# Five of eight blocks of the last layer's output projection as filler of the stick-breaking steps, whose tiles run from the last to the first

## What is computed

```
h = x @ w_in                      # split into q, k, v, gates of three mixers
o_nsa = nsa_mixer(...)            # 6 heads, columns 0:384
o_sb  = stick_breaking_mixer(...) # 4 heads, columns 384:640
o_hg  = hgrn2_mixer(...)          # 6 heads, columns 640:1024, a recurrence over the tokens
mixed = concat([o_nsa * silu(nsa_z), o_sb * silu(sb_z), norm(o_hg) * silu(hg_z)])
x = layer_norm(ALPHA * x + mixed @ w_out, ln_g, ln_b)
```

## Time and profile before

| | |
|---|---|
| median of 3 runs | 1381.4 us (1378.87 to 1387.62) |
| the profiled execution | 1383.62 us, its span 1381.8 us |
| mean granted TensorE clock | 0.925 |
| PE busy | 1223.5 us (89%) |
| DVE busy | 552.5 us (40%) |
| ACT busy | 427.6 us (31%) |
| POOL busy | 112.5 us (8%) |

### The profile page before, as it was taken

One profiled execution on the slowest core, in us unless ns is written; L12 is line 12 of the kernel. 1 busy time (PEld: TensorE's weight loads), 2 busy tenths in 40 slices (PEclk: granted clock), 3 DMA queues, 4 the chain that ended last, 5 costly groups with the idle time before them and its releaser, 6 DMA issues.

```text
span 1381.8 us, 15110 instructions
## 1 busy us (share of the span) xinstructions
PE 1223.5 (89%) x5264; PEld 684.8 (50%) x5264; DVE 552.5 (40%) x1422; ACT 427.6 (31%) x1086; POOL 112.5 (8%) x140
## 2 busy tenths in 40 slices
PE   4879989999898899979999989989999899867974
PEld 1555454455564444334455555555454556445541
DVE  3234323333544320334443432112225632758871
ACT  0133013444451101222234321114344544651211
POOL 0000000000002000000000000000000000574722
PEclk8889989999998999999999999999999999856997
DMA  9321234463002422332111005241101111000000
GB/s 347 105 92 31 93 127 177 160 226 73 0 1 70 77 38 61 70 111 61 62 61 61 1 11 137 62 167 46 46 1 46 46 62 62 1 3 30 1 32 30
DMA packets 60258, 99.71 MB, mean 72 GB/s; under 512 B 12068, under 2 KB 22129, under 8 KB 60184
## 3 DMA queue, kind: packets, MB, share of 16 engines
q1 hardware_dynamic: 54370, 93.58, 21.9%
q10 hardware_dynamic: 5814, 5.18, 1.2%
HBM read 96.60 MB, written 4.08 MB: 73 GB/s over the span
## 4 chain that ended last, share of the span: by engine, by line
PE 75%; DVE 13%; ACT 6%; issue 2%; DMA 2%; ACTq 1%; POOL 0%; DVEq 0%; SPq 0%; POOLq 0%
PE PR L867 33%; PE OB L897 6%; PE PT L779 6%; PE SC L919 6%; PE PR L779 5%; PE OB L779 4%; PE SC L779 4%; PE PT L934 3%; PE PR L960 3%; DVE stage L1677 2%; DMA ring<-in_w_ada 2%; DVE d L1677 1%; DVE tok L1677 1%; DVE arena L1893 1%; PE PT L867 1%
## 5 line engine op out<-in xcount | busy, mean ns | idle before, releaser
L867 PE MATMUL PR<-ring,hT 128*128 128x512 f32 (+1 forms) x784 | 381.7, 600 | 4.8 <-ACT hT L1208 4.0
L867 PEld LDWEIGHTS PR<-ring,hT 128*128 128x128 f32 x784 | 137.7, 199 | 105.0 <-issue 87.8
L1367 ACT ACTIVATE stage<-stage,nmax 128x256 f32<-128x256 f32 (+7 forms) x200 | 103.7, 519 | 264.7 <-DVE nmax L2023 233.5
L897 PEld LDWEIGHTS OB<-arena,pts 128*128 128x128 f32 (+3 forms) x880 | 133.1, 202 | 99.9 <-issue 76.8
L867 PE MATMUL PR<-hT,ring 128*128 128x512 f32 (+1 forms) x304 | 149.9, 616 | 0.0
L1585 POOL TENSOR_TENSOR arena<-arena 128x192 f32<-128x192 f32 (+1 forms) x118 | 80.1, 679 | 798.3 <-PE OB L897 749.5
L897 PE MATMUL OB<-arena,pts 128*128 128x64 f32 (+4 forms) x880 | 131.4, 279 | 11.5 <-ACT pts L1208 11.5
L919 PE MATMUL SC<-arena 64*128 64x256 f32 (+15 forms) x432 | 114.9, 459 | 10.2 <-DVE nmax L2023 10.2
L934 PEld LDWEIGHTS PT<-ident,stage 128*128 128x128 f32 (+3 forms) x440 | 59.1, 147 | 110.7 <-issue 69.0
L934 PE MATMUL PT<-ident,stage 128*128 128x128 f32 (+3 forms) x440 | 87.2, 290 | 24.6 <-ACT stage L1339 11.8
L1208 ACT ACTIVATE pts<-PT 128x256 f32<-128x256 f32 (+7 forms) x200 | 80.9, 404 | 84.0 <-PE PT L934 62.4
(11 more groups left out here) (337 smaller groups left out, 1288.5 us busy)
## 6 DMA issues: line engine op xcount, KB each, us to landing
ring<-in_w_ada SPq DMA_DIRECT2D x12, 2048.0 KB, 8.3
ring<-in_od_w_in SPq DMA_DIRECT2D x8, 2048.0 KB, 16.7
ring<-in_w_in SPq DMA_DIRECT2D x5, 1536.0 KB, 6.9
ring<-in_ev_w_in SPq DMA_DIRECT2D x3, 2048.0 KB, 7.7
ring<-in_w_in SPq DMA_DIRECT2D x3, 2048.0 KB, 10.0
ring<-in_ev_w_out SPq DMA_DIRECT2D x2, 2048.0 KB, 10.2
ring<-in_od_w_out SPq DMA_DIRECT2D x2, 2048.0 KB, 8.0
ring<-in_w_out SPq DMA_DIRECT2D x2, 2048.0 KB, 7.7
```

Of the source, the lines that this page charges most:

```text
L867: mm = pe.matmul(dst, l, r, start=(k == 0), stop=(k == KT - 1))
L897: mm = pe.matmul(ob[:, h * w:h * w + w], pts[0:rows_, v % 2, n * P:n * P + P], vb, start=(n == 0), stop=(n == len(blocks) - 1))
L1367: give(act.activation(pb[:, s % NP, 0:n], zm[:, s % 2, 0:n], ACT.Exp, bias=nmax[:, row, c:c + 1], scale=-1.0, accum_out=rsum[:, row, c:c + ...
```

## The change

Two things are done together.

1. The first five blocks of each tile's output projection leave `output_tile`. For each tile they become four jobs, `heads_ahead(i)`: `mE` 0 and 1 transpose the five finished blocks (4 and 1) and ACT copies them back into `tok`; `ye` 0 and 1 are the two halves of five products each, and DVE's `residual_ahead` writes `ALPHA * x + product` into `x`. Tiles 3, 2 and the first three jobs of tile 1 are filler of steps 78 to 87; tile 1's last job runs between attention and the tail; tile 0's four run beside c = 0 of the tail. `output_tile` keeps three transposes, one ACT copy and twice three products, and `residual_half` becomes a plain addition.
2. The stick-breaking groups run tile 3, 2, 1, 0 (`STICK_ORDER`). The earlier filler is moved into fewer steps: 21 tiles in steps 0 to 64, `hi` in steps 65 to 77. `HG_EARLY` stays (78, 84).

```diff
+EARLY = 5
+STICK_ORDER = (3, 2, 1, 0)
+def heads_ahead(i):
+    return [("mE", i, 0), ("mE", i, 1), ("ye", i, 0), ("ye", i, 1)]
...
-     (("w", "hi"), [("hi", i) for i in range(T)])],
+     (("w", "hi"), [("hi", i) for i in range(T)]),
+     (("wo", 2, 0), []),
+     (("wo", 2, 1), heads_ahead(3) + heads_ahead(2) + heads_ahead(1)[:3])],
...
-[(21, 68), (4, 14)]]
+[(21, 65), (4, 13), (2, 1), (2, 3), (2, 1), (2, 3), (2, 1), (1, 1)]]
...
+    jobs.append(("ye", 1, 1))
     for c in range(T + 1):
         if c < T - 1:
             jobs.append(("kbT", c))
         if c:
-            jobs.extend([("mT", 2, c - 1, 0), ("mT", 2, c - 1, 1), ("y", 2, c - 1, 0), ("y", 2, c - 1, 1)])
+            jobs.extend([("mT", 2, c - 1, 0), ("y", 2, c - 1, 0), ("y", 2, c - 1, 1)])
+        else:
+            jobs.extend(heads_ahead(0))
...
-OUT_SPREAD = [8, 4, 4, 8]
+OUT_SPREAD = [[5, 4, 3, 0], [3, 2, 2, 2]]
...
+                if kind == "mE":
+                    i, g = name[1:]
+                    if g == 0:
+                        pe.wait_ge(ob_free, g_no[2, 3 * T + STICK_ORDER.index(i)] + 1)
+                    transposes(name, [tok[:, i, k * P:k * P + P] for k in ((4,) if g else range(4))])
+                if kind == "ye":
+                    for g in range(2):
+                        freed(pe, ("mE", i, g))
+                    for k in range(EARLY):
+                        mm = pe.matmul(b[:, :], tok[:, i, k * P:k * P + P], W[:, k, :], ...)
...
-            drained(pe, ("hi", T - 1))
+            whole_tile(("ye", 1, 1))
             pe.wait_ge(ob_free, len(g_no))
...
+            def mixed_ahead(i, g):
+                b = take(act, ("mE", i, g))
+                release(copy(tok[:, i, 4 * P * g:4 * P * g + w], b[:, 0:w]), ("mE", i, g))
...
+            def residual_ahead(i, h):
+                b, w = take(dve, ("ye", i, h)), slice(512 * h, 512 * h + 512)
+                release(stt(x[:, i, w], x[:, i, w], ALPHA, b[:, :], ALU.mult, ALU.add), ("ye", i, h))
...
-                release(stt(ybuf2[:, i % 2, w], x[:, i, w], ALPHA, b[:, :], ALU.mult, ALU.add), ("y", 2, i, h))
+                release(tt(ybuf2[:, i % 2, w], x[:, i, w], b[:, :], ALU.add), ("y", 2, i, h))
...
-                    if c and m == 0:
-                        mixed_half(c - 1)
+                    if c == 0 and m == 0:
+                        residual_ahead(1, 1)
...
                 if c:
                     residual_half(c - 1, 0)
+                else:
+                    for h in range(2):
+                        residual_ahead(0, h)
```

More of the change, by code:

```diff
@@ L293, in attention_plan @@
             groups += [(kind, i, [[(kind, h, i)] for h in row_halves(NSH)]) for kind in ("cmp", "sel", "win")]
-        groups += [("sb", i, [[("sb", h, i)] for h in range(SBH)]) for i in range(T)]
+        groups += [("sb", i, [[("sb", h, i)] for h in range(SBH)]) for i in STICK_ORDER]
     return groups
-OUT_SPREAD = [8, 4, 4, 8]
+OUT_SPREAD = [[5, 4, 3, 0], [3, 2, 2, 2]]
 RING = 3
@@ L338, in two_block_kernel @@
     for name in jobs:
-        few = name in beside or name[0] in ("kbT", "st") or name[:2] in (("mT", 2), ("y", 2))
+        few = name in beside or name[0] in ("kbT", "st", "mE", "ye") or name[:2] in (("mT", 2), ("y", 2))
         b = turn[few] % (2 if few else 8)
@@ L943, in output_tile @@
             def output_tile(i):
[L945 to L955, removed]
+                b = begin(("mT", 2, i, 0))
+                for k in range(EARLY, KT):
+                    if k == EARLY:
+                        pe.wait_ge(hof, i + 1)
+                    tr = pe.transpose(b[:, (k - EARLY) * P:(k - EARLY + 1) * P], tok[:, i, k * P:k * P + P], ident[:, :])
+                    if k == KT - 1:
+                        tr.then_inc(pr_done, 1)
+                    yield
+                freed(pe, ("mT", 2, i, 0))
                 for h in range(2):
@@ L958, in output_tile @@
                     b = begin(("y", 2, i, h))
-                    for k in range(KT):
-                        mm = pe.matmul(b[:, :], hT[:, k, i * P:i * P + P], W[:, k, :], start=(k == 0), stop=(k == KT - 1))
+                    for k in range(EARLY, KT):
+                        mm = pe.matmul(b[:, :], hT[:, k, i * P:i * P + P], W[:, k, :], start=(k == EARLY), stop=(k == KT - 1))
                         if k == KT - 1:
@@ L1151, in outputs @@
                     mm.then_inc(ho_done, 1)
-                beside_it = output_tile(c - 1) if c else iter(())
+                beside_it = output_tile(c - 1) if c else (None for name in heads_ahead(0) for _ in tile_matmuls(name))
                 def feed(k):
-                    for _ in range(OUT_SPREAD[k]):
+                    for _ in range(OUT_SPREAD[min(c, 1)][k]):
                         next(beside_it, None)
@@ L1554, in _ @@
                     b = take(act, ("mT", 2, c - 1, 0))
-                    release(copy(hT[:, 0:4, (c - 1) * P:c * P], heads(b[:, :])), ("mT", 2, c - 1, 0))
+                    release(copy(hT[:, EARLY:KT, (c - 1) * P:c * P],
+                                 b[:, 0:384].rearrange("p (j t) -> p j t", j=KT - EARLY)), ("mT", 2, c - 1, 0))
+                else:
+                    for g in range(2):
+                        mixed_ahead(0, g)
                 if 1 <= c < T - 1:
@@ L1872, in tile_done @@
                     next(chains[-1])
+                elif kind == "ye":
+                    residual_ahead(*name[1:])
                 elif kind == "mT" and i == 1:
@@ L2228, in output_tile @@
                 give(ts(yb, yb, lam[:, 7:8], ALU.add, rr[:, 0:1], ALU.mult), ln_s, i + 1)
[L2230 to L2233, removed]
             def residual_half(i, h):
@@ L2293, in _ @@
             output_tile(T - 2)
-            mixed_half(T - 1)
             residual_half(T - 1, 0)
```

23 lines of the change are left out of this document (18 added, 5 removed).

## The result

| | before | changed kernel |
|---|---|---|
| median of 7 runs each, side by side | 1383.74 us (1378.83 to 1387.63) | 1391.2 us (1389.96 to 1397.69) |
| ratio, 95% interval | | 1.0069 [1.0051, 1.0086] |
| profiled execution, its span | 1383.62, 1381.8 us | 1390.36, 1388.6 us |
| mean granted clock | 0.925 | 0.931 |

The changed kernel is slower by 0.7%: the interval leaves 1 out, and the difference is less than the 1% that the prediction counted as telling. The forecast was 1388. Its span, 1388.6, is to the tenth that of the profiled execution, but this one is the second shortest of the seven; the median lies 3.2 us above the forecast, and the kernel before came out 2.3 us above the median that the forecast started from. By the ratio the change cost 9.5 us, where +6.8 was forecast.

The account below looks back on a forecast made before the run. The DVE-ACT ping-pong and POOL's chain were taken to bound the stick-breaking steps, mostly DVE the tail. +17.8 + 7.9 - 4.8 - 14.1 = +6.8 us gave 1388 us against the median 1381.4; 8 in 10 range 1369 to 1404.

Parts of the forecast that it names:

- Part 1: Before step 72: eight more filler products cost 5.2 us, longer scores of three units +1.9.
- Part 2: Step 72 to end of step 78: ping-pong sets the pace, PE's work is hidden; exponentials 0 start about 1210.4, 16.5 us later.
- Part 3: Steps 79 to tail: late POOL makes ACT stand some 5 us before exponentials 1 at 1238.7; whole stick-breaking part +17.8 us.
- the slower rival: Clock stays at 1.2 GHz through the `ye` filler: +17 on the forecast, 1405; chance 0.25.
- two signs of failure: Prediction fails if ACT meets no wait at step 84, or something other than the ping-pong paces the stick-breaking steps.
- the ping-pong: Stick-breaking steps: DVE and ACT alternate, unit r + 2's mask awaiting unit r's last exponential; period 4.57 us for 512 keys.
- Part 4: Tail, c = 0: waiting for a bank DVE frees, added products and a lower clock make 22 us of 14.1, +7.9.
- Part 5: Tail, c = 1 to 3: each loses DVE's 0.69 us copy into `hT`; -3.1, -0.7 and -1.0 us.
- Part 6: After the last tile's recurrence: 10.4 us instead of 24.5, six products 7.7 mostly at the lower clock; -14.1 us.
- Faster: Stick-breaking steps: POOL and ACT are done before PE needs them, the fill covers the gaps; 1365 to 1378, chance 0.20.
- No effect: Whole kernel: the work moved is hidden at both ends; inside the forecast's own range, no separate chance.

Follow-up runs that it names:

- v6: Changed kernel with tiles 1 and 2 left in the tail; tile 3's jobs in the steps, tile 0's beside c = 0: 1378.03 us, ratio 0.9970.
- v1: Kernel before, order and filler kept, only tile 3's four jobs made ahead, all beside c = 0: 1366.69 us, ratio 0.9892.
- v5: Kernel before, order reversed, tile 3's first three jobs in steps 82 to 87, its last beside c = 0: 1369.66 us, ratio 0.9905.
- e4: Changed kernel with other products placed between a tile's transposes and its own products: 1391.77 us, ratio 1.0058.
- e3: Changed kernel with exponentials 0 at the end of step 75 instead of 78: 1394.46 us, ratio 1.0075.
- e1: Kernel before with only the stick-breaking tiles reversed: 1382.52 us, ratio 1.0006.
- v3: Kernel before, tile 3's first three jobs beside c = 0, its last beside c = 2, tile 0's four in steps 82 to 87: 1366.39 us, ratio 0.9891.
- e2: Changed kernel with DVE's residual_ahead(1, 1) before the tail's loop, not after the first combination: 1387.03 us, ratio 1.0023.
- v2: Kernel before, only tile 3's jobs made ahead, the first three beside c = 0, the last beside c = 2: 1365.35 us, ratio 0.9882.
- v4: Kernel before, order reversed, old filler kept, only tile 3's four jobs ahead, in steps 82 to 87: 1366.26 us, ratio 0.9902.

## Why the prediction was right, and where it wasn't

**Part 1, the filler moved up.** Forecast were +5.2 for the filler and +1.9 for the scores, together 7.1. The changed kernel's profile alone shows +3.5; the twelve in groups show +6.0 and +2.0. The eight extra products in a stretch without a gap cost about what their durations say, and v6, which still pays them (and 6.1 us more in c = 0), is the one reduced version that stays behind v1 to v5.

**Part 2, the long steps first.** Exponentials 0 begin at 1208.95; 1210.4 was forecast. The error is in two terms that go against each other: P came 3.6 us earlier than forecast in this profile, and from P to the exponentials it took some 2 us longer.

**Part 3, the step that failed.** The forecast had POOL late and ACT standing still for 5 us in front of exponentials 1. ACT met no wait there, and it was POOL that stood still, for 7.51 us. Three terms were off. POOL took 22.3 us (21.37 and 0.83, with its gaps), not 24.5, so it was done at 1235.19, not 1238.7. ACT came at 1238.73, not 1234. And what follows exponentials 1 took 15.1 us (1242.55 to 1257.67), not 17.6, since the last ten products ran in about 9.2 us, near full clock, not mostly at the lower one. ACT was late because PE was: the sum for steps 79 to 84 had the products' durations and no term for the two waits for ACT's copies (2.72 and 2.73 us), nor for the six records behind each, which took 2.05 + 3.62 us where six take some 2.7 at full clock. That is 5.45 and about 6 us, more than the 4.7 us by which ACT was late, and no run took the waits away (e4 meant to and didn't, v6 keeps the first of them), so what each is worth is not shown. The forecast saw exactly this wait in c = 0 and in the slower rival's sentence, and left it out of the sum of the steps. An error of 3.5 us (POOL) and one of 4.7 (ACT) met at the same number, 1238.7, and the exponentials began there by luck. Of the two signs of failure that the prediction named for itself, the first came true outright (ACT met no wait at step 84). So did the second, in the steps after exponentials 0: not the ping-pong paced them but PE (DVE waits there for PE's scores, line 951, up to 6.9 us at a time). That the total was near doesn't make that step right. e3 settles which of the two it was: with POOL done 16.8 us ahead, nothing moved.

The mechanism isn't wrong as such. It is there in e1, v5 and v6 (ACT waits 2.50, 3.69 and 1.91 us). It needs PE to be quick, and with the new products PE isn't.

By the Trainium skill (SBUF — State Buffer, "SBUF: two separate sides"), named in Part 3, a POOL instruction that reads SBUF and a DVE instruction with two SBUF inputs exclude each other. POOL's 31 instructions took 26.9 us with the tiles in the old order and 22.3 in the changed kernel. Of the stretch of the first 30, DVE was busy 18.11 of 25.97 us before, 14.64 of 24.34 in v3, 13.70 of 21.57 in e1 and 10.94 of 21.37 in the changed kernel. POOL's first 15 took 10.22 us in the old order and 13.30 in e4, now beside the long steps. That agrees with the rule; no run here changed DVE's work alone.

**Part 4, c = 0.** +7.68, forecast +7.9, by the steps named: the wait for DVE's release (3.35 us) and the lower clock after it (six records in 4.83 us). e2 takes the wait away and gets 5.85 us back, so the cause is shown.

**Part 5.** c = 1 gained 2.95, forecast 3.1. c = 2 and c = 3 were to gain 0.7 and 1.0 and gained nothing (-0.13, +0.28). The step that failed is "each loses DVE's copy": DVE lost 0.69 us of work, but at c = 2 it now waits 1.14 us for PE's level products.

```profile
1312.30 1.09 DVE L1718 TENSOR_TENSOR stage<-SC,grow 128x896 f32<-128x896 f32 x1 [1.14 <-PE SC L1160]
```

PE has less to do in the tail and does it more slowly: clock 0.76 instead of 0.84. By the Trainium skill (TensorE: Matmul & The Clock Gate, "HAM oscillation — how this bites in real kernels") it is the pauses between groups of products that bring the clock down. The windows agree: PE was idle for 12.7 of 88 us before and for 35.3 of 84 us after.

At c = 3 DVE waits for PE no more than before. What takes the gain is mainly one small DVE instruction: 0.17 us long before, it takes 1.77 beside an instruction of POOL's layer norm, and ends 0.02 us after it.

```profile
1334.59 2.34 POOL L1626 TENSOR_TENSOR x<-ring,arena 128x1024 f32<-128x1024 f32 x1
```

```profile
1335.18 1.77 DVE L1718 TENSOR_TENSOR rt<-rr 128x6 f32<-128x6 f32 x1 [0.64 <-ACT rr L1243]
```

It is as long (1.79) in e2, e3 and e4, where tiles 1 and 2 are ahead too, and 0.17 us in e1 and v1 to v6. Another (`d<-d`, 128x384) met POOL more before (1.56 us) than now (0.99). The two together are +1.0 us, against the 0.69 that the copy gave back. The forecast had no term for such meetings.

**Part 6, the end.** -13.67, forecast -14.1; six products in 8.40 us, forecast 7.7. The forecast priced the lower clock as given, since PE has paused. v1 shows that it wasn't: the pause (7.89 us) is made by the change itself, and where tile 2 keeps its eight blocks the same end takes 7.94 instead of 10.86 us (v1, v2, v4 to v6).

**The rivals.** Faster: its condition came true (POOL needed 22.3 us, ACT met no wait for it) and its result didn't, since PE took over as the bound. Slower: PE's clock from 1212 to 1258 was 0.89, so the `ye` filler didn't stay at the lower clock; in the steps mainly the records after the two waits ran at it. No effect: the interval, 1.0069 [1.0051, 1.0086], and the table speak against it, though the size is within the forecast's 1%.

**What stays open.** Whether the two waits in the steps go away with a third bank, and what that would bring. Why v3's last products took 7.05 us after only 1.28 us of idle PE, where v1's took 5.42 after 0.93. Why e1's 3.4 us from P to the tail don't show in its time; the 2.0 us that its order seems to cost before P and 0.7 in c = 0 are most of it, if single profiles can be trusted so far.

## What to carry to other kernels

Move ahead only the work whose end is exposed: of four tiles one paid (tile 3, some 16 us), one gained nothing in the steps and lost 3 us beside c = 0 (tile 0), and two cost 10.4 us, because only 5.7 us of the added work fell into PE's gaps. When a fill consists of dependent jobs (transpose, copy by another engine, product), count its waits and the bank that each job holds, not only its products. And when a total comes out right, look whether each engine did what the sum said: here a late POOL was forecast and a late PE was found, and only the second tells what to change.

## What the runs showed of the hardware

- Relieving PE in a stretch that another engine paces can cost at the next place where PE does set the end: the granted clock of the tail went from 0.84 to 0.76, and the last twelve records from 5.42 us (v1) to 8.40.
- The length of the last idle time alone doesn't tell the clock behind it. After 2.72 us the next two records of 128x512 took 2.05 us and four more 3.62 (changed kernel), after 2.83 us 1.38 and 3.13 (e4). The last twelve took 5.42 us in v1, after 0.93 and 0.64 us of idle time around the transposes, and 7.05 us in v3, after 1.28 and 0.64.
- POOL's 30 instructions of 128x192 took 25.94 to 25.97 us in the profiles of before, v1 and v2, 24.34 in v3, which has the same order with other work in the last steps, and 21.37 to 22.79 in the eight with the order reversed. So their length goes with the work that stands beside them: DVE was busy 18.11 us beside them before, 14.64 in v3 and 10.94 in the changed kernel.
- A DVE instruction of 128x6 took 0.17 us in eight profiles and 1.77 to 1.79 in the four where it ran beside POOL's layer norm, ending within 0.03 us of the POOL instruction beside it.
